# Retrieval stage of a two-block transformer kernel: products and sums of the index look-ups on GpSimd, weight splits placed between other steps of a pick

## The reference, cut to what matters

```python
q = (xc @ w_pq).reshape(P_CHUNK, P_HEADS, 2, P_DK // 2)          # 8 heads, 2 halves
s = jnp.einsum('thpd,hpkd->thpk', q, sub_keys)                   # 128 keys per half
s_top, i_top = lax.top_k(s, P_TOPK)                              # 16 of 128
cand = s_top[..., 0, :, None] + s_top[..., 1, None, :]
best, ci = lax.top_k(cand.reshape(P_CHUNK, P_HEADS, P_TOPK * P_TOPK), P_TOPK)
e1 = jnp.take_along_axis(i_top[..., 0, :], ci // P_TOPK, axis=-1)
e2 = jnp.take_along_axis(i_top[..., 1, :], ci % P_TOPK, axis=-1)
expert = e1 * N_KEYS + e2
gate = jax.nn.softmax(best)
act = gelu(einsum('thkd,td->thk', u_tab[expert], xc))
out = einsum('thk,thkd->td', gate * act, v_tab[expert])
```

## Time and profile before

| | |
|---|---|
| median of 3 runs | 3275.33 us (3273.89 to 3276.46) |
| the profiled execution | 3275.38 us |
| its span in the profile | 3273.7 us |
| TensorE busy over the span | 3156.6 us, 96% |
| VectorE busy | 2430.2 us, 74% |
| ScalarE busy | 1441.6 us, 44% |
| GpSimd busy | 259.2 us, 8% |
| mean granted TensorE clock | 0.99 |

### The profile page before, as it was taken

The page is one execution under the profiler, slowest core; times in us unless marked ns, Lnnn a source line. Parts: engine busy times, 40 slices in busy tenths (PEclk is TensorE's granted clock), DMA queues, the critical chain, the costliest instruction groups (busy, mean ns, idle before and its releaser), DMA issues.

```text
span 3273.7 us, 45409 instructions
## 1 busy us (share of the span) xinstructions
PE 3156.6 (96%) x16031; PEld 2594.5 (79%) x16031; DVE 2430.2 (74%) x4442; ACT 1441.6 (44%) x2477; POOL 259.2 (8%) x238
## 2 busy tenths in 40 slices
PE   7999999999999999999999999999999999999998
PEld 4786667789899999999988876767888766678886
DVE  5997776779988968888888878876656566674344
ACT  5336774243344444444444445474323256543232
POOL 0000000000000113333322200000000000000000
PEclk9999999999999999999999999999999999999999
DMA  6242115633356789999999966522556522123222
GB/s 247 90 148 68 68 65 187 230 99 128 123 185 183 214 283 355 372 373 367 372 392 368 382 233 158 133 65 97 187 192 194 166 79 78 46 92 102 97 97 78
DMA packets 151163, 604.94 MB, mean 185 GB/s; under 512 B 16029, under 2 KB 25885, under 8 KB 133695
## 3 DMA queue, kind: packets, MB, share of 16 engines
q1 hardware_dynamic: 98080, 363.13, 32.0%
q0 software_dynamic: 34672, 207.89, 17.5%
q10 hardware_dynamic: 18222, 31.42, 3.7%
HBM read 550.74 MB, written 51.65 MB: 184 GB/s over the span
## 4 chain that ended last, share of the span: by engine, by line
PE 74%; DVE 14%; ACT 4%; DMA 3%; issue 2%; DVEq 2%; PEld 0%; ACTq 0%; PEldq 0%; SPq 0%; POOL 0%; POOLq 0%
PE ps L432 16%; PE ps L434 16%; PE ps L433 16%; PE ps L2861 5%; PE ps L2860 5%; PE ps L2859 5%; DVE w_lo L415 2%; PE ps L2896 1%; PE ps L2730 1%; DVE A L2170 1%; PE ps L2707 1%; DMA raw<-w_all 1%; DVE B L2173 1%; DMA mod_up<-w_mods 1%; ACT w_hi L410 1%
## 5 line engine op out<-in xcount | busy, mean ns | idle before, releaser
L432 PE MATMUL ps<-RH,w_hi 128*128 128x512 f32 (+1 forms) x2464 | 921.8, 374 | 25.6 <-DVE w_lo L415 9.7
L415 DVE TENSOR_TENSOR w_lo<-raw,w_hi 128x1024 fp32r<-128x1024 f32 x535 | 654.7, 1224 | 344.3 <-ACT w_hi L410 331.5
L434 PE MATMUL ps<-RH,w_lo 128*128 128x512 f32 (+1 forms) x2464 | 907.7, 368 | 0.0
L433 PE MATMUL ps<-RL,w_hi 128*128 128x512 f32 (+1 forms) x2464 | 907.3, 368 | 0.0
L410 ACT ACTIVATE w_hi<-raw 128x1024 fp32r<-128x1024 f32 x535 | 564.6, 1056 | 587.6 <-PE ps L434 371.5
L432 PEld LDWEIGHTS ps<-RH,w_hi 128*128 128x128 f32 x2464 | 465.0, 189 | 107.8 <-issue 27.4
L433 PEld LDWEIGHTS ps<-RL,w_hi 128*128 128x128 f32 x2464 | 465.1, 189 | 57.7 <-issue 1.9
L434 PEld LDWEIGHTS ps<-RH,w_lo 128*128 128x128 f32 x2464 | 464.9, 189 | 57.6
L2861 PE MATMUL ps<-w_hi,WL 128*128 128x512 f32 x768 | 299.8, 390 | 0.0
L2860 PE MATMUL ps<-w_lo,WH 128*128 128x512 f32 x768 | 299.7, 390 | 0.0
L2859 PE MATMUL ps<-w_hi,WH 128*128 128x512 f32 x768 | 298.9, 389 | 0.0
(11 more groups left out here) (398 smaller groups left out, 4221.5 us busy)
## 6 DMA issues: line engine op xcount, KB each, us to landing
raw<-w_all SPq DMA_DIRECT2D x536, 512.0 KB, 3.6
mod_in<-w_modr SPq DMA_DIRECT2D x112, 512.0 KB, 4.3
peer_gate_scratch<-Gs POOLq DMA_DIRECT2D x12, 2048.0 KB, 12.2
GL<-peer_gate_scratch POOLq DMA_DIRECT2D x32, 768.0 KB, 8.1
act_scratch<-act_out ACTq DMA_DIRECT2D x76, 192.0 KB, 2.7
act_in<-act_scratch POOLq DMA_DIRECT2D x19, 768.0 KB, 10.0
mod_up<-w_mods SPq DMA_DIRECT2D x4, 2048.0 KB, 18.8
mod_two<-w_modr SPq DMA_DIRECT2D x8, 1024.0 KB, 6.9
```

Of the source, the lines that this page charges most:

```text
L415: nc.vector.tensor_tensor(w_lo[j][:], raw[j][:], w_hi[j][:].bitcast(F32), ALU.subtract).then_inc(lo_done, 1)
L432: nc.tensor.matmul(out_ap, w_hi[slot][:, k, :], rh, start=start and x == 0, stop=False)
L433: nc.tensor.matmul(out_ap, w_hi[slot][:, k, :], rl, start=False, stop=False)
L434: last = nc.tensor.matmul(out_ap, w_lo[slot][:, k, :], rh, start=False, stop=stop and x == n - 1)
```

## The change

The comparison of each look-up stays on VectorE and now writes one of four buffers `found[h % 2][x]`. The product with the indices and the sum over 16 are made by GpSimd, in a loop ahead of its gate loop: it waits on `half_ready`, which each comparison raises, multiplies in place, and adds halves, 8 + 8, 4 + 4, 2 + 2 and 1 + 1, the last into `E`, with a drain ahead of each. After both look-ups of a head it raises `look_done`. The index tables `top_f` and the positions `half_f` have two sets, by head. VectorE waits for `look_done` in two places: ahead of the copy into `top_f` of a pick with m = 0 from the third head on (for the head two before), and after the last pick, ahead of the softmax, for all eight heads. `breaks` goes from 15 to 10 for the picks with m = 1: the units lie between the steps up to the positions, and the last one behind the comparisons.

```diff
--- before.py
+++ after.py
@@ -240,14 +240,16 @@
         left = at(S + 12, "left", [P, TB, NK])
         cand = at(S + 14, "cand", [P, TB, WIDE + LONG])
         cand2 = at(S + 18, "cand2", [P, TB, WIDE + LONG])
-        hit = at(S + 22, "hit", [P, TB, 256])
         top_v = [at(S + 26 + m / 4, f"top_v{m}", [P, TB, TOPK]) for m in range(2)]
         top_i = [at(S + 26.5 + m / 4, f"top_i{m}", [P, TB, TOPK], U32) for m in range(2)]
-        top_f = [at(S + 27 + m / 4, f"top_f{m}", [P, TB, TOPK]) for m in range(2)]
+        top_f = [[at(S + kb + m / 4, f"top_f{q}_{m}", [P, TB, TOPK]) for m in range(2)] for q, kb in enumerate((27, 30))]
         best = at(S + 27.5, "best", [P, TB, TOPK])
         best_i = at(S + 27.75, "best_i", [P, TB, TOPK], U32)
         half_i = [at(S + kb, f"half_i{m}", [P, TB, TOPK], U32) for m, kb in enumerate((28, 28.25, 29.5, 29.75))]
-        half_f = [at(S + 28.5 + m / 4, f"half_f{m}", [P, TB, TOPK]) for m in range(2)]
+        half_f = [[at(S + kb + m / 4, f"half_f{q}_{m}", [P, TB, TOPK]) for m in range(2)]
+                  for q, kb in enumerate((28.5, 30.5))]
+        found = [[at(S + kb, f"found{q}_{m}", [P, TB * TOPK, TOPK]) for m, kb in enumerate(pair)]
+                 for q, pair in enumerate(((22, 64), (68, 72)))]
         zsum = at(S + 29, "zsum", [P, TB * PEER_H])
         zmax = at(S + 29.25, "zmax", [P, TB * PEER_H])
         E = [at(S + 76 + 2 * m, f"E{m}", [P, TB, PEER_H, TOPK]) for m in range(3)]
@@ -358,6 +360,7 @@
         wo_evac, pw_evac, out_evac, m_hi = sem("wo_evac"), sem("pw_evac"), sem("out_evac"), sem("m_hi")
         m_lo = sem("m_lo")
         gate_in, gate_in2 = sem("gate_in"), sem("gate_in2")
+        half_ready, look_done = sem("half_ready"), sem("look_done")
         q_ready, sc_done, sc_evac = sem("q_ready"), sem("sc_done"), sem("sc_evac")
         z_ready = sem("z_ready")
         e_tp, hot_done, g_mm, g_evac = sem("e_tp"), sem("hot_done"), sem("g_mm"), sem("g_evac")
@@ -826,6 +829,21 @@
             pool.drain()
             g.affine_select(out=ident[:], in_=ident[:], compare_op=ALU.not_equal, fill=1.0, base=0,
                             pattern=[[-1, P]], channel_multiplier=1).then_inc(consts_made, 1)
+
+            for h in range(PEER_H):
+                for x in range(2):
+                    pool.wait_ge(half_ready, 2 * h + x + 1)
+                    f = found[h % 2][x]
+                    fb = f[:].rearrange("p (b x) y -> p b x y", b=TB)
+                    g.tensor_tensor(fb, fb, top_f[h % 2][x][:].unsqueeze(2).to_broadcast([P, TB, TOPK, TOPK]), ALU.mult)
+                    n = TOPK // 2
+                    while n > 1:
+                        pool.drain()
+                        g.tensor_tensor(f[:, :, 0:n], f[:, :, 0:n], f[:, :, n:2 * n], ALU.add)
+                        n //= 2
+                    pool.drain()
+                    ins = g.tensor_tensor(E[x][:, :, h, :], fb[:, :, :, 0], fb[:, :, :, 1], ALU.add)
+                ins.then_inc(look_done, 1)
 
             with pool.Fori(0, GI) as i:
                 for b in range(2):
@@ -1533,11 +1551,13 @@
                 for b in range(TB):
                     v.max_index(top_i[m][:, b, 8:16], top_v[m][:, b, 8:16], left[:, b, :])
                 dve.drain()
-                v.tensor_copy(top_f[m][:], top_i[m][:])
+                h = g // 2
+                if m == 0 and h >= 2:
+                    dve.wait_ge(look_done, h - 1)
+                v.tensor_copy(top_f[h % 2][m][:], top_i[m][:])
                 if m == 0:
                     return
 
-                h = g // 2
                 splits(3)
                 for lo, n, x0, x1, y in ((0, WIDE, 0, 4, TOPK), (WIDE, LONG, 4, TOPK, 4)):
                     v.tensor_tensor(cand[:, :, lo:lo + n].rearrange("p b (x y) -> p b x y", y=y),
@@ -1568,37 +1588,31 @@
                 v.tensor_single_scalar(half_i[3][:], best_i[:], 12, ALU.bitwise_and)
                 v.tensor_copy(E[2][:, :, h, :], best[:])
                 dve.drain()
-                v.scalar_tensor_tensor(half_f[0][:], half_i[2][:], -12.0, half_i[0][:], ALU.add, ALU.max)
-                v.scalar_tensor_tensor(half_f[1][:], best_i[:], float(WIDE), half_i[3][:], ALU.is_lt, ALU.mult)
+                half = half_f[h % 2]
+                v.scalar_tensor_tensor(half[0][:], half_i[2][:], -12.0, half_i[0][:], ALU.add, ALU.max)
+                v.scalar_tensor_tensor(half[1][:], best_i[:], float(WIDE), half_i[3][:], ALU.is_lt, ALU.mult)
                 dve.drain()
-                v.tensor_tensor(half_f[1][:], half_f[1][:], half_i[1][:], ALU.add)
-
+                v.tensor_tensor(half[1][:], half[1][:], half_i[1][:], ALU.add)
                 for x in range(2):
                     if x:
                         dve.drain()
-                    v.tensor_tensor(hit[:].rearrange("p b (x y) -> p (b x) y", y=TOPK),
-                                    half_f[x][:].rearrange("p b x -> p (b x)").unsqueeze(2).to_broadcast(
+                    v.tensor_tensor(found[h % 2][x][:],
+                                    half[x][:].rearrange("p b x -> p (b x)").unsqueeze(2).to_broadcast(
                                         [P, TB * TOPK, TOPK]),
-                                    iota[:, 0:TOPK].unsqueeze(1).to_broadcast([P, TB * TOPK, TOPK]), ALU.is_equal)
-                    dve.drain()
-                    splits(9 + 3 * x)
-                    hb = hit[:].rearrange("p b (x y) -> p b x y", y=TOPK)
-                    v.tensor_tensor(hb, hb, top_f[x][:].unsqueeze(2).to_broadcast([P, TB, TOPK, TOPK]), ALU.mult)
-                    dve.drain()
-                    splits(10 + 3 * x)
-                    v.tensor_reduce(E[x][:, :, h, :], hit[:].rearrange("p b (x y) -> p b x y", x=TOPK),
-                                    AX.X, ALU.add)
-                    dve.drain()
-                    splits(11 + 3 * x)
+                                    iota[:, 0:TOPK].unsqueeze(1).to_broadcast([P, TB * TOPK, TOPK]),
+                                    ALU.is_equal).then_inc(half_ready, 1)
+                for b in range(9, breaks):
+                    splits(b)
 
             for j in range(RING):
                 lo_ahead(dve, R_PQ, j)
             for i in range(1, 4):
-                for j, (k0, k1, breaks) in enumerate(((0, 1, 3), (1, 6, 15), (6, 7, 3), (7, 12, 15))):
+                for j, (k0, k1, breaks) in enumerate(((0, 1, 3), (1, 6, 10), (6, 7, 3), (7, 12, 10))):
                     pick(RING * i - RING + j, R_PQ + 3 * i - 2, k0, k1, breaks)
-            for j, (k0, k1, breaks) in enumerate(((0, 1, 3), (1, 10, 15), (10, 11, 3), (11, 20, 15))):
+            for j, (k0, k1, breaks) in enumerate(((0, 1, 3), (1, 10, 10), (10, 11, 3), (11, 20, 10))):
                 pick(12 + j, R_UP, k0, k1, breaks)
 
+            dve.wait_ge(look_done, PEER_H)
             bv = E[2][:].rearrange("p b h k -> p (b h) k")
             v.tensor_copy(zmax[:], bv[:, :, 0])
             dve.drain()
```

## The result

The changed kernel takes 3286.45 us (median of 7 runs, 3282.25 to 3288.25) against 3275.98 us for the kernel before on the same chip: ratio 1.0032, 95% interval [1.0021, 1.0042]. It is **slower by 10.5 us**; 3273.3 had been forecast, and 3286.45 lies 3.45 above the range. The profiled execution took 3282.25 us (span 3280.6), so it is the quickest of the seven, 6.9 above the one of before.

The account below looks back on a forecast made before the run. The prediction took VectorE to bound the retrieval stage, making TensorE lose 15.1 us. Its terms, -15.1 + 10.6 + 2.5 = -2.0 us, took 3275.33 to 3273.3 us; range 3266 to 3283.

Parts of the forecast that it names:

- I take x below that, so 15.1 stands: Retrieval stage: overlap loss per head assumed under 3.8 us, so TensorE never waits and regains all 15.1 us.
- x: What VectorE's overlapped splits and comparisons lose per head beside GpSimd's work; between 0 and 5.9 us.
- 15.1: Microseconds TensorE loses against its own pace before the meeting after retrieval; forecast to come back in full.
- the bounds of 0 to 5.9: Range of VectorE's overlap loss per head: from none to the GpSimd instructions in front, 2.35 + 1.2 + 2.35 us.
- the limit of 3.8: Overlap loss per head, in us, below which six heads of excess fit into the 12.5 us lead.
- 12.5 us of lead: VectorE's splits run three units ahead of TensorE in the retrieval stage, covering 12.5 us.
- Moving them is worth nothing by itself while three units of lead cover it: Splits moved closer to the pick's early steps: no effect by itself; without lead a late split costs up to 1.2 us.
- GpSimd's tables: GpSimd's product and sums for one look-up: 5.7 us per table, ends 3.0 and 8.8; 11.4 us per head.
- The row that was trusted for x: Profile row of VectorE's subtraction beside a GpSimd select: 0.73 us against 0.69 alone, 0.04 lost.
- The rival built on it: Engines exclude each other at the second comparison and two splits of each head: 5.9 us lost per head, 3288.7 us; chance 0.12.
- The new wait at the end: Last head's look-ups, under no next pick: TensorE idles from 961.9 to 973.65, transposes 4.5 us earlier, half clock 2.5 us.
- -15.1 + 10.6 + 2.5: Forecast total: TensorE's loss returned, idle time at the meeting added, half clock behind it added; -2.0 us.

Follow-up runs that it names:

- experiment 3: The changed kernel with GpSimd making fills that read nothing in place of its product and sums, look-up result left out: 3271.12 us.
- experiment 5: The changed kernel with the split behind the comparisons moved ahead of them and GpSimd released only after a head's second comparison: 3279.60 us.
- 10: The changed kernel with comparisons behind the last split, GpSimd released after both, last head's look-ups on VectorE, and two units in pick 12: 3262.09 us.
- experiment 6: The changed kernel with comparisons behind the last split, GpSimd released after both, and the last head's look-ups on VectorE with 15 places: 3265.99 us.
- 1: The kernel before with only the splits' places of the change (10 instead of 15), look-ups all on VectorE: 3287.43 us.
- 8: The kernel before with look-ups on VectorE and 10 places for the splits, but the first head keeping 15: 3281.76 us.
- 7: The changed kernel with 15 places for the splits in the first head alone: 3281.92 us.
- experiment 12: The changed kernel with one set of buffers, VectorE waiting for the look-ups of the head just before: 3291.61 us.
- Experiments 2: The changed kernel with the last head's look-ups made by VectorE, with 15 places in that pick: 3272.14 us.
- 4: The kernel before with only the last head's look-ups on GpSimd, with the change's places in that pick: 3287.67 us.

## Why the prediction was wrong, point by point

- **"I take x below that, so 15.1 stands" is the step that failed, and within it the lead.** 3.4 of the 15.1 came back. Measured x, 3.0 to 4.1 and 3.5 in the mean, lies inside the bounds of 0 to 5.9 and in the mean even under the limit of 3.8: six heads run 6 x 1.75 = 10.5 us behind, and by the forecast's own test 12.5 us of lead would have kept TensorE free of waits. It first waited when VectorE had fallen back by only 3.7 (797.55). So x had been left without a value where it needed one, and the 12.5 that it was held against were not there. That contention is needed for the loss is shown by experiment 3: the same places and about the same occupation of GpSimd without its reading, and TensorE never waits. Of the 11.7 left, 6.5 go when the comparisons are kept apart from GpSimd (5), and 4.9 more when pick 12 has a second unit (10 less 6); 0.3 remain. The single unit in that pick stands in the kernel before and in experiment 3 too, and in 3 TensorE crosses it without a wait.
- **"Moving them is worth nothing by itself while three units of lead cover it" is false too.** The lead of 12.5 us was taken as given, but it is made in the first head, while TensorE is slow, and only if VectorE gets ahead there; splits placed early make it wait for ScalarE, 10.65 us instead of 4.3. That is 6.35 of the 12.5. How much of the rest was missing through the uneven places of the splits, as in pick 12, no run tells. With the look-ups on VectorE the places cost 12 us (1), 6 of them in the first head (1 less 8). Within the change their share is smaller, since other things take the place of that cost: with the first head's places back (7) the loss is 10.3 and the time 4.5 us less, because there two splits fall under GpSimd's tables and lose 3.2 us between them, and the second one waits 1.7 for ScalarE. The two causes, contention and the shortened lead, can't be priced one by one and added.
- **The row that was trusted for x was too small to show it.** A subtraction that lost 0.04 us beside a select of 0.29 was set against one slow select. The rule of the Trainium skill (SBUF — State Buffer, "Who interferes with whom"), that a VectorE instruction with two SBUF inputs and a GpSimd instruction that reads SBUF exclude each other for the whole instruction, agrees with the measured 3.46 and 2.30 us in place of 1.22 and 1.23, and with the fills of experiment 3, which read nothing and held up neither comparisons nor splits. By it the bound x = 5.9 would have been the value to take; the measured one is lower because the next pick's split meets GpSimd in three of six heads only, and then one of the sums (0.8 to 1.1 us lost, not 2.35). The rival built on it gave 3288.7, 2.25 from the result, and had 0.12. Its mechanism is shown, but the nearness of its figure is in part luck: it took x = 5.9 and a whole lead, where x is 3.5 and the lead at least half gone.
- **GpSimd's tables were right.** 5.7 us a table was worked out; alone it takes 5.67 (experiment 6, 791.64 to the end at 797.31). (The select's row, 0.29 us, gives 1.5 ns per element and not the 1.54 used; that would take under 0.2 us off a table.) With 1.2 for standing behind VectorE the last head was to take 12.6 from its release, and took 12.87 (961.55 to 974.42).
- **The new wait at the end was right, and its size nearly.** TensorE was to idle 11.75 us and idled 10.27. The chain from the softmax's first step (974.46) to the transposes took 8.2, not 10.0: ScalarE loads its table at 965.01, while it waits, and VectorE then stands 0.7 us for the exponentials, where it stood 2.9 in the kernel before. The half clock cost 1.9 and not 2.5. But all this was set off against 15.1 us given back, and only 3.4 came: the comparison of the last head ended 10.5 us later than forecast (961.47 against 950.95), the tables with it, 974.42 against 963.65.
- **The second buffers** had been worked out as what keeps pick h + 1 from waiting; experiment 12 agrees, with 1.4 us a head.
- **The sum.** -15.1 + 10.6 + 2.5 was forecast. Against before the measured terms are -3.4, +9.1 and +1.9, with -1.2 from stages ahead and 0.5 unexplained: +6.9. The median is 3.6 us above that. The profiled execution had a mean clock of 0.988, five of the other six 0.985 to 0.987, and the kernel before 0.990: the rest goes along with a lower mean clock. Where and why is open. Experiments 2 and 3 differ from the change, and 4 from the kernel before, by 3, 4 and 1 us more than loss, gap and clock account for, so most of it seems to sit in the change.

## What to carry to other kernels

Before work goes from VectorE to GpSimd, list VectorE's two-input instructions that can meet it and price each as if it waited for a whole GpSimd instruction (here 2.2 us behind a product, 1.1 behind a sum); start GpSimd after them, not between them. A lead is a stock that is filled somewhere: before steps are moved, find where, and what an early step would stand waiting for. Leave the last piece of such a chain, which nothing hides, on the quick engine. Here the order of experiment 5, the last head on VectorE and one split more in pick 12 turn 3286 us into 3262, 0.4% under the kernel before.

## What was not expected of the hardware

- Against a running GpSimd product even VectorE's copy of 64 unsigned integers per partition to floats, one input, took 1.98 us instead of 0.20 (792.10, experiment 6; 1.98 again at 881.05), and against fills up to 0.86 (experiment 3). Searches and maxima with one input, 0.28 us each, were not longer in the same stretches.
- GpSimd pays as well: its three larger sums took 4.29 us with VectorE's instructions between them and 2.69 without (794.18, experiment 6).
- GpSimd fills of 1024 elements, 0.96 us each in the mean, left VectorE's comparisons (2.54 for two) and splits (1.22) as they were and kept their own length beside them.
